# Dense products of one transformer kernel as pairs of 64-row matmuls, with evictions and sums ordered by pairs

## What is computed

```python
def first_block(x, ...):
    proj = rms_norm(x, pre_mix_g) @ w_in          # q, k, v | rwkv | gates
    ...                                            # band attention, rwkv7 mixing
    x = x + rms_norm(merged @ w_out, post_mix_g)
    hf = rms_norm(x, pre_ffn_g)
    u = jnp.square(jax.nn.relu(hf @ w_up)) @ w_down        # 1024 -> 4096 -> 1024
    x = x + rms_norm(u, post_ffn_g)

# then an even layer (mLSTM and forgetting attention) and an odd layer (SSD and pooling):
#   in = x @ w_in_2 ; mixed = ... ; x = layer_norm(ALPHA * x + mixed @ w_out_2)
#   h = causal_dwconv(x @ ffn_w_up_2, 3 taps)     # 1024 -> 2 x 2816
#   x = layer_norm(ALPHA * x + (value * sigmoid(gate) * gate) @ ffn_w_down_2)
```

## Time and profile before

| what | value |
|---|---|
| median of three runs | 2378.5 us |
| the profiled execution, its own time | 2376.1 us |
| its span in the trace | 2374.3 us |
| mean granted TensorE clock | 0.94 of 2.4 GHz |
| TensorE, matmuls busy | 2198.3 us (93%) |
| VectorE, ScalarE, GpSimd busy | 1024.0, 818.6, 831.6 us |
| DMA | 183 MB, 23% of 16 engines |

### The profile page before, as it was taken

The page is one execution under the profiler, slowest core; times in us unless marked ns, Lnnn a source line. Parts: engine busy times, 40 slices in busy tenths (PEclk is TensorE's granted clock), DMA queues, the critical chain, the costliest instruction groups (busy, mean ns, idle before and its releaser), DMA issues.

```text
span 2374.3 us, 29768 instructions
## 1 busy us (share of the span) xinstructions
PE 2198.3 (93%) x12446; PEld 1773.2 (75%) x12454; DVE 1024.0 (43%) x1648; ACT 818.6 (34%) x1241; POOL 831.6 (35%) x367
## 2 busy tenths in 40 slices
PE   4999889999799999989998799999989888999997
PEld 4767678888678888867776678888867467888886
DVE  3023874544541022246337644442248564444323
ACT  3343421134343133232335254443233334444322
POOL 3423310014444444443231244444443124444441
PEclk8999988799899999999999899999989988999998
DMA  5322100014223323212111122323312112232321
GB/s 215 102 80 85 54 28 2 3 33 146 71 70 99 98 89 104 96 58 75 50 54 45 53 67 94 98 98 98 98 53 80 36 45 68 92 101 94 102 94 53
DMA packets 52862, 182.97 MB, mean 77 GB/s; under 512 B 5609, under 2 KB 5617, under 8 KB 52601
## 3 DMA queue, kind: packets, MB, share of 16 engines
q1 hardware_dynamic: 52728, 181.08, 23.0%
HBM read 176.32 MB, written 7.62 MB: 77 GB/s over the span
## 4 chain that ended last, share of the span: by engine, by line
PE 84%; DVE 12%; ACT 1%; DMA 1%; issue 1%; POOL 0%; SPq 0%; ACTq 0%; DVEq 0%
PE ps L315 19%; PE ps L316 19%; PE ps L317 19%; PE ps L1363 3%; PE ps L414 2%; PE ps L2298 2%; PE ps L2300 1%; PE ps L2299 1%; PE ps L331 1%; PE ps L933 1%; PE ps L332 1%; PE ps L420 1%; PE ps L333 1%; PE ps L2834 1%; DVE work L1489 1%
## 5 line engine op out<-in xcount | busy, mean ns | idle before, releaser
L177 POOL TENSOR_TENSOR split_units<-raw_units,split_units 128x1024 fp32r<-128x1024 f32 x314 | 762.8, 2438 | 1444.4 <-ACT split_units L168 1444.4
L315 PE MATMUL ps<-x_split,split_units 128*128 128x512 f32 x1344 | 529.2, 394 | 13.0 <-POOL split_units L177 12.2
L316 PE MATMUL ps<-x_split,split_units 128*128 128x512 f32 x1344 | 525.0, 391 | 0.0
L317 PE MATMUL ps<-x_split,split_units 128*128 128x512 f32 x1344 | 524.5, 390 | 0.0
L168 ACT ACTIVATE split_units<-raw_units 128x1024 fp32r<-128x1024 f32 x314 | 329.4, 1052 | 428.0 <-PE ps L317 381.6
L315 PEld LDWEIGHTS ps<-x_split,split_units 128*128 128x128 f32 x1344 | 253.6, 189 | 70.7 <-POOL split_units L177 12.8
L316 PEld LDWEIGHTS ps<-x_split,split_units 128*128 128x128 f32 x1344 | 253.6, 189 | 53.5 <-issue 1.7
L317 PEld LDWEIGHTS ps<-x_split,split_units 128*128 128x128 f32 x1344 | 253.5, 189 | 53.3
L315 PE MATMUL ps<-hidden_split,split_units 128*128 128x512 f32 x608 | 237.3, 390 | 0.0
L317 PE MATMUL ps<-hidden_split,split_units 128*128 128x512 f32 x608 | 236.6, 389 | 0.0
L316 PE MATMUL ps<-hidden_split,split_units 128*128 128x512 f32 x608 | 236.5, 389 | 0.0
(11 more groups left out here) (406 smaller groups left out, 3192.8 us busy)
## 6 DMA issues: line engine op xcount, KB each, us to landing
raw_units<-stream SPq DMA_DIRECT2D x314, 512.0 KB, 3.5
bias_rows<-bias_line SPq DMA_DIRECT2D x1, 2816.0 KB
gate_rows<-work SPq DMA_DIRECT2D x10, 256.0 KB, 2.1
work<-gate_rows SPq DMA_DIRECT2D x10, 256.0 KB, 2.7
x<-x_t SPq DMA_DIRECT2D x4, 512.0 KB, 5.4
work<-bias_rows SPq DMA_DIRECT2D x1, 2048.0 KB
out_t<-x SPq DMA_DIRECT2D x8, 256.0 KB
vec<-vectors SPq DMA_DIRECT2D x1, 1163.5 KB, 11.5
```

The source lines that it names most:

```text
L177: gpsimd.tensor_tensor(self.split[:, u % SPLIT, 1, :], self.raw[:, u % RING, :], self.split[:, u % SPLIT, 0, :].bitcast(F32), ALU.subtract ...
L315: TE.matmul(out, high, rhs(0, k), start=(k == 0), stop=False)
L316: TE.matmul(out, high, rhs(1, k), start=False, stop=False)
L317: ins = TE.matmul(out, low, rhs(0, k), start=False, stop=last)
```

## The change

1. A tile's K = 128 blocks are split into an upper half (rows 0 to 63 of the array and of the input's partitions) and a lower half (64 to 127). Tiles go in pairs: one matmul uses the upper half of the array for one tile of the pair, the next the lower half for the other, each into its own bank. For each block position there are two passes: straight (upper half on tile a, lower on tile b), then crossed.
2. Tiles go in fours: first passes of pair 0, of pair 1, then second passes of pair 0, of pair 1 (four slots of time). Both tiles of a pair are complete at the same moment. `first_products` becomes `first_four`, which does the first passes of both pairs together.
3. The three matmuls of a block become three pairs of 64-row matmuls: the number of instructions doubles, the number of multiplications stays. The weight stream is laid out anew on the host (`halves_of_pairs`), a unit is still 8 blocks and is used for one slot when a tile has 8 blocks.
4. The lists of ScalarE and VectorE are reordered: evictions of a pair together, then joins, sums and squares; the roundings ahead of them as the slots release units (`slot_units`). `factor_pe` starts the sums of x before the last squares are there. Side jobs of `stage_even_in` and `stage_odd_in` move to the ends of fours, and in the even layer the four turned tiles stand together.

```diff
+        def half_products(pe, pair, part, k, rhs, start, stop):
+            high, low = wts.take(pe)
+            outs = [(bank(2 * pair), half(part)), (bank(2 * pair + 1), half(1 - part))]
+            for weights, x_half in ((high, 0), (high, 1), (low, 0)):
+                done = [TE.matmul(out, weights[rows], rhs(x_half, k)[rows], start=start and weights is high and x_half == 0,
+                                  stop=stop and weights is low) for out, rows in outs]
+            return done
...
+        def four_tiles(pe, n, order, rhs, free=None, ready=None, late=None):
+            firsts = []
+            for pair in range(2):
+                if free is not None:
+                    free(pe, 2 * pair)
+                firsts.append(first_half(pe, pair, order, rhs, ready))
+                ready = None
+            for pair in range(2):
+                second_half(pe, pair, order, rhs, firsts[pair], n + 2 * pair, late if pair else None)
...
+        def slot_units(u0, m, n_k=UNIT, ahead=0):
+            slots = (m & ~3) + (3 if m % 4 < 2 else 4) - ahead
+            return u0 + slots * n_k // UNIT + SPLIT
```

`first_half` issues `half_products` with part 0 over the blocks, `second_half` with part 1, and the latter raises `tile_ready` once for each tile of the pair; `free` waits until both tiles that last held the pair's banks have been read. The evictions of the later feed-forwards, and of the products with a sum behind them:

```diff
                 for m in range(2 * FF2):
-                    wts.round_high(act, S, u0 + m + SPLIT)
+                    wts.round_high(act, S, slot_units(u0, m, ahead=1))
...
-                    if m % 2 == 0 and m >= 2:
+                    if m % 2 and m >= 3:
                         gate(m // 2 - 1)
...
                 for m in range(2 * FF2):
                     conv(m)
-                    if m % 2 == 0 and m >= 2:
+                    if m % 2 and m >= 3:
                         join(m // 2 - 1)
...
+                for m in range(0, KD, 2):
+                    if centre:
+                        shifted = [shift_mean(t) for t in (m, m + 1) if t]
+                    if sums is not None and m >= 2:
+                        add_square(m - 1)
+                    if centre:
+                        dve.wait_ge(dve_chain.sem, shifted[-1])
+                    if m or not centre:
+                        evict(m)
+                    if centre and m == KD - 2:
+                        add_x(m)
+                    evict(m + 1)
+                    for t in (m, m + 1) if centre and m < KD - 2 else ():
+                        if t:
+                            add_x(t)
+                    if sums is not None and m >= 2:
+                        add_square(m)
```

The even layer's list of jobs:

```diff
-              ("tile", 19), ("turn", 0), ("turn", 1), ("tile", 20), ("turn", 2), ("turn", 3), ("tile", 21),
+              ("tile", 19), ("turn", 0), ("turn", 1), ("turn", 2), ("turn", 3), ("tile", 20), ("tile", 21),
               ("tile", 22), ("tile", 23))
```

More of the change, by code:

```diff
@@ L116, in link, with at @@
         eng.wait_ge(self.sem, self.mark(ins))
+    def at(self, n):
+        return n
 class Weights:
@@ new lines, in four_tiles, with first_four @@
+        def four_tiles(pe, n, order, rhs, free=None, ready=None, late=None):
[7 more added lines that the diff above has]
+                second_half(pe, pair, order, rhs, firsts[pair], n + 2 * pair, late if pair else None)
+        def first_four(pe, rhs, before, between=None, late=None):
+            order = before.order
+            before.pe(pe)
+            for i, k in enumerate(order):
+                before.ready(pe, k)
+                last = i == len(order) - 1
+                for pair in range(2):
+                    done = half_products(pe, pair, 0, k, rhs, i == 0, False)
+                    if last and pair:
+                        wts.free(done[1], halves_done, halves_done.n + 1)
+                    else:
+                        wts.free(done[1])
+            first = halves_done.mark(done[1])
+            if between is not None:
+                between(pe)
+            for pair in range(2):
+                second_half(pe, pair, order, rhs, first, 1 + 2 * pair, late if pair else None)
@@ L2936, in blocks, with halves_of_pairs @@
     return m.reshape(k // P, P, n // P, P).transpose(2, 0, 1, 3).reshape(-1, P, P)
+def halves_of_pairs(m, order=None, together=False):
+    n, n_k = m.shape[:2]
+    if order is not None:
+        m = np.concatenate([m[:4, list(order)], m[4:]])
+    pairs = m.reshape(n // 4, 2, 2, n_k, 2, HD, P)
+    straight = np.stack([pairs[:, :, 0, :, 0], pairs[:, :, 1, :, 1]], axis=3)
+    crossed = np.stack([pairs[:, :, 1, :, 0], pairs[:, :, 0, :, 1]], axis=3)
+    out = np.stack([straight, crossed], axis=1).reshape(n // 4, 2, 2, n_k, P, P)
+    parts = []
+    for i, four in enumerate(out):
+        first = four[0].transpose(1, 0, 2, 3) if together and i == 0 else four[0]
+        parts += [first.reshape(-1, P, P), four[1].reshape(-1, P, P)]
+    return np.concatenate(parts)
 def weight_stream(a):
```

278 lines of the change are left out of this document (154 added, 124 removed).

## The result

| | before | after |
|---|---|---|
| median | 2378.7 us (2378.2 to 2380.3, 4 runs) | 2424.2 us (2417.4 to 2426.3, 4 runs) |
| profiled execution, its own time | 2376.1 us | 2417.4 us |
| its span | 2374.3 us | 2415.6 us |
| mean granted clock | 0.94 | 0.94 |

The ratio is 1.0185 with a 95% interval of 1.0165 to 1.0206: the changed kernel is 46 us slower where 25 us less were forecast. The profiled execution of it was the fastest of its four, so its trace holds 41 us of the 46; how its time varies from one execution to the next is told under run 5.

A forecast was written before the change was run, and what follows sets the result against it. TensorE's matmuls bound most stretches, VectorE the odd input and even output. Savings of 16.4 + 11.3 + 8.5 + 1.8 = 38.0 us less 12.6 lost gave 25.4: 2351 from the profiled execution, 2353 us as median; range 2332 to 2406.

The forecast's parts named there:

- step 1: Pace of the converted matmuls: a pair takes 216 ns, saving 16.4, 11.3 and 8.5 us where TensorE is the bound.
- step 2: Later up projections: new waits in each four leave 1.8 us saved instead of 22.6; at the old pace 4.2 us lost.
- (a): Ends of products: the last two tiles complete together, so evictions and squares delay what follows; 2.6 us lost together.
- (d): Odd input: first tiles complete 5.4 us later, but pairs hide 8.4 us of sigmoid waits; 0, between -3 and +5 us.
- step 3: What the new order of tiles costs at several stages: 12.6 us lost in sum.
- A pair runs as one: Two 64-row matmuls on alternating halves of the array run together, so doubling the instructions costs little or nothing.
- the prediction's own sign: Up projections: TensorE waits once or twice in a four; no such wait means that step 2 is wrong.
- (b): Even output: VectorE's chain starts after three slots instead of after one and the mean's matmul; 3 us lost.
- (c): Even input: more VectorE work stands ahead of the copy the last four tiles wait for; 6 us of 0 to 9.
- (e): Changes between 64-row and full matmuls inside products may drain the array, at some eight places; 1 us lost.
- Same pace: Rival for all converted matmuls: the fp32r pair takes 226.7 ns like the full matmul; 2395 us, chance 0.24.
- Slower pace: Rival for all converted matmuls: the pair is 2 to 10 ns slower; 2421 us, chance 0.10.

The follow-up runs named there:

- run 5: The changed kernel with the third weight unit of the later down projections rounded right after the last eviction, ahead of the last two joins: 2417.8 us, ratio 1.0172.
- Run 2: The kernel before with half of the 4096-wide feed-forward in other matmul forms (fewer columns, 64 rows, bf16), sums wrong: 2351.4 us, only distances between starts read.
- run 4: The kernel before with only the early sums: behind linear layers the sums of x start before the last square is there: 2374.6 us, ratio 0.9989.
- run 6: The changed kernel with the input of the odd layer put back as before, full matmuls tile after tile: 2411.5 us, ratio 1.0143.
- Runs 1, 11 and 12: The changed order with full 128-row matmuls: 2414.4 us; then, on one chip, the changed kernel again, 2418.9 us, and the full-matmul fours again, 2417.0 us.

## Why the prediction was wrong

The forecast was 2353 us and the time 2424, 71 us more. By the stage times of the two profiles 36 of them are step 1, 3 the up projections of step 2, 10 the down projections, and 19 the terms (a) to (d) of step 3; some 5 lie in the other executions, slower than the profiled one, and smaller differences of 2 us go the other way.

**A pair runs as one: right.** The second matmul of a pair mostly starts 3 to 17 ns behind the first, and no stretch shows twice the time.

**Step 1, the pace: the step that failed first.** It took 216 ns for a pair because "the missing 13 ns belong to the 4-byte stream into 128 rows". Run 2 shows a fixed price of 13 to 14 ns for each fp32r matmul, paid with 64 rows as with 128, and the pair in the changed kernel takes 226.1 to 226.8 ns. Nor does it follow from the load lying under the matmul that the load has no part in the 13 ns; run 2 leaves that open. The nearest row in form, the float32 pair of the earlier trace rows, had said that nothing is gained; I set a bf16 row against it that shows another type, not another number of rows. 36.2 us of the sum went there. The table of the Trainium skill (TensorEngine Tiling (Array Packing), Theoretical Speedup) that the prediction weighed gives a factor only where a dimension is 64 or less. The trace agrees: the product over 128 rows cut in two took as long as before, 86.81 us for 384 pairs or 384 full matmuls.

**Step 2, waits in the up projections: too dark.** It asked for 0.19 us a four at the old pace, 4.2 us in 22 fours. The two up projections lost 1.4 us, and TensorE shows no wait inside them, where one or two in a four were forecast: by the prediction's own sign step 2 is wrong. The two chains fit where it had them late by a tenth or two; which of its durations was too long was not looked into. But the same list of ScalarE has its price at the end of the stage, which I did not follow: the third unit of the down projection is rounded behind the last join. That wait and the clock behind it are 4.3 us a layer (run 5), a term that the sum doesn't have.

**Step 3, the order: the step that failed as well. 12.6 us were forecast, about 31 measured in its four terms.**
(a) The ends of products were put at 2.6 us; without the even output, which is (b), the norms behind five products are 10 us longer. The start of the sums moved by 0.76 us behind four of them (2.71 instead of 1.95 us), with a layer norm as without one. With a layer norm the early sums had won 0.7 us where tiles come singly (1.24 us in run 4), and the pair of evictions took that back and as much again: the last tile is read later, and the sums of x need that tile, so that no square covers it. Behind the odd output VectorE was late by another 2 us. Its list has eight operations of 0.69 us for a pair there, 5.5 us, and a pair of 8-block tiles leaves it one slot of 5.4 us; that this is the reason is read from the list, not tested. And the clock: 3.2 us there, 1.2 behind w_out.
(b) The even output, 3 us: right, 3.3.
(c) The even input, 6 us of 0 to 9: 8.6 with the mixing behind it, at the upper end. The mechanism is there: the last four tiles start 72.3 us after the stage's first matmul, and 73.4 were reckoned.
(d) The odd input, 0 between -3 and +5: wrong, +9.0, and by run 6 most of it is this stage's own. The step had the first tiles 5.4 us late; they came 13.8 us late, because the side product of 7 us, which lay beside VectorE's first tiles, now lies ahead of them.
(e) Changes of mode, 1 us: no run shows the term by itself. Runs 1, 11 and 12 leave 2 to 5 us for all that the form costs.

**The rivals.** *Same pace* had the mechanism of the pace, at 0.24, and was right that step 1 is zero. Its price of 16.8 us was the same sum of steps 2 and 3, and so short by 29 us; its 2395 us was as wrong as its terms. *Slower pace*, at 0.10, gave 2421 us, 3 from the median, and that is luck: the pair is not slower, and what it put down to the pace is the order. The range ended at 2406, and no rival asked what happens if the order alone is dearer than reckoned. That a wait also costs clock was in no term: the trace of the kernel before has norms with sums at either clock, and I did not ask which side a wait of 2.7 us falls on. In the traces it falls on either.

## What to carry to other kernels

Before a form of instruction is used for its pace, measure the pace in a form that differs from the old one in nothing else; here one run with a few forms settled what the rewriting of 2048 blocks was staked on. When tiles are completed in groups, look at who works first: in the odd input VectorE bounds the stage, its first tile came 13.8 us later, and the stage took 9 us more, because a side job that was hidden beside its work no longer was. A wait of TensorE is to be reckoned with what it does to the clock behind it, and short waits around norms were worth filling here.

## What the runs showed of the hardware

- An fp32r matmul, with its weight load, has a fixed price of 13 to 14 ns beyond its columns at 2.4 GHz (120.6 ns for 256, 226.7 for 512 columns), with 64 rows as with 128; a bf16 matmul some 2.5 ns (109.3 and 216 ns).
- Two 64-row matmuls on different halves of the array run as one: 215.9 ns a pair of 512 columns in bf16, 226.1 to 226.8 ns in fp32r. That is what one 64-row matmul takes alone (216 and 227.3 ns), and what one of 128 rows takes.
- Behind 2.7 us from the last matmul the same sums ran at a granted clock of 1.00 in one execution and 0.52 in another, the code of the stage being the same; behind 4.8 us at 0.50. Filling the waits around the norms with unused matmuls made the kernel before 0.7% faster, 0.1% of it by the early sums.
